# Half tiles of the hi and lo weight ring 2064 bytes apart in place of 2048

## The reference, cut to what matters

```python
split(xn @ w_in)                                   # 4096 x 5456 with the gate's low-rank part
for o, wb in zip((o_a, o_b, o_c, o_d), split(w_branch)):
    gate = sigmoid((z @ gate_up[i]))               # 256 x 4096 each
    merged = merged + gate * (o @ wb)              # 512 (or 256) x 4096 each
h = h + merged @ w_out                             # 4096 x 4096
q = xn2 @ wq                                       # 4096 x 1024
act = gelu(xn2 @ u.T)                              # 4096 x 4096
h = h + wmat @ v                                   # 4096 x 4096
```

## Time and profile before

| | |
|---|---|
| median of 2 runs | 1907.89 us (1907.87 to 1907.91) |
| span of the profiled execution, first to last instruction | 1906.1 us |
| TensorE matmul busy | 1900.6 us, 8941 recorded |
| TensorE weight load busy | 1567.2 us, 8941 recorded |
| VectorE busy | 1463.9 us |
| ScalarE busy | 984.9 us |
| TensorE's granted clock | 1.000 on average |

### The profile page before, as it was taken

How to read it: one execution, slowest core, us unless ns; L and a number is a source line. 1 busy time by engine, 2 the same in 40 slices (tenths; PEclk the granted TensorE clock), 3 DMA queues, 4 the chain that set the end, 5 groups by cost and what they waited for, 6 DMA issues and landing times.

```text
span 1906.1 us, 25847 instructions
## 1 busy us (share of the span) xinstructions
PE 1900.6 (100%) x8941; PEld 1567.2 (82%) x8941; DVE 1463.9 (77%) x2139; ACT 984.9 (52%) x1214; POOL 36.2 (2%) x49
## 2 busy tenths in 40 slices
PE   9999999999999999999999999999999999999999
PEld 8888888888888888888888888888887788888887
DVE  7578775584556889889765555899988878999897
ACT  6653644445456655546454464444444455555553
POOL 0010010000000000000000000000000000000000
PEclk9999999999999999999999999999999999999999
DMA  9976666655655668877887776767766668666664
GB/s 326 344 226 166 172 174 199 176 156 157 191 177 178 185 190 288 278 226 238 254 256 234 216 226 218 232 208 221 219 201 198 197 208 290 223 213 218 210 219 155
DMA packets 198832, 412.69 MB, mean 217 GB/s; under 512 B 45792, under 2 KB 124256, under 8 KB 198080
## 3 DMA queue, kind: packets, MB, share of 16 engines
q1 hardware_dynamic: 174048, 369.35, 63.0%
q10 hardware_dynamic: 20976, 25.19, 3.9%
q0 software_dynamic: 3696, 16.65, 2.4%
HBM read 390.15 MB, written 20.97 MB: 216 GB/s over the span
## 4 chain that ended last, share of the span: by engine, by line
PE 97%; DVE 2%; DMA 0%; issue 0%; ACT 0%; SPq 0%; DVEq 0%; ACTq 0%
PE acc L676 25%; PE acc L679 25%; PE acc L683 25%; PE acc L724 3%; PE acc L726 3%; PE acc L730 3%; PE side L1039 1%; PE side L1038 1%; PE acc L1152 1%; PE side L1040 1%; PE acc L1079 1%; PE acc L1085 1%; PE side L854 1%; PE acc L1080 1%; PE side L966 1%; DVE w_lo L1608 1%
## 5 line engine op out<-in xcount | busy, mean ns | idle before, releaser
L1608 DVE TENSOR_TENSOR w_lo<-w_raw,w_hi 128x1024 fp32r<-128x1024 f32 (+1 forms) x649 | 785.6, 1214 | 389.7 <-ACT w_hi L1199 384.9
L1199 ACT ACTIVATE w_hi<-w_raw 128x1024 fp32r<-128x1024 f32 (+1 forms) x649 | 681.1, 1052 | 701.2 <-PE acc L683 577.5
L676 PE MATMUL acc<-w_hi,xt_hi 128*128 128x512 f32 x1348 | 365.7, 393 | 0.0
L679 PE MATMUL acc<-w_hi,xt_lo 128*128 128x512 f32 x1348 | 360.8, 390 | 0.0
L683 PE MATMUL acc<-w_lo,xt_hi 128*128 128x512 f32 x1348 | 360.6, 389 | 0.0
L679 PEld LDWEIGHTS acc<-w_hi,xt_lo 128*128 128x128 f32 x1348 | 253.1, 188 | 53.1
L683 PEld LDWEIGHTS acc<-w_lo,xt_hi 128*128 128x128 f32 x1348 | 253.1, 188 | 52.9
L676 PEld LDWEIGHTS acc<-w_hi,xt_hi 128*128 128x128 f32 x1348 | 250.2, 188 | 51.5 <-issue 1.8
L676 PE MATMUL acc<-w_hi,x_hi 128*128 128x512 f32 x640 | 175.1, 396 | 0.0
L679 PE MATMUL acc<-w_hi,x_lo 128*128 128x512 f32 x640 | 171.5, 390 | 0.0
L683 PE MATMUL acc<-w_lo,x_hi 128*128 128x512 f32 x640 | 171.4, 390 | 0.0
(11 more groups left out here) (376 smaller groups left out, 2061.5 us busy)
## 6 DMA issues: line engine op xcount, KB each, us to landing
w_raw<-in_stream SPq DMA_DIRECT2D x504, 512.0 KB, 4.2
w_raw<-in_w_in SPq DMA_DIRECT2D x16, 496.0 KB, 4.1
w_raw<-in_w_in SPq DMA_DIRECT2D x16, 480.0 KB, 3.9
w_raw<-in_w_in SPq DMA_DIRECT2D x16, 464.0 KB, 3.8
w_raw<-in_w_in SPq DMA_DIRECT2D x16, 448.0 KB, 3.9
w_raw<-in_w_in SPq DMA_DIRECT2D x16, 432.0 KB, 3.9
w_raw<-in_w_in SPq DMA_DIRECT2D x16, 416.0 KB, 4.0
w_raw<-in_w_in SPq DMA_DIRECT2D x16, 400.0 KB, 3.8
```

The lines of the kernel that those rows point to most:

```text
L676: pe.matmul(o[h], lhs(k0 + j, h)[0], wh[j], start=first and j == 0, stop=False)
L679: pe.matmul(o[h], lhs(k0 + j, h)[1], wh[j], start=False, stop=False)
L1199: nc.scalar.activation(w_hi[:, slot, 0:width], w_raw[:, slot, 0:width], ACT.Copy).then_inc(hi_ready, 1)
L1608: nc.vector.tensor_tensor(w_lo[:, slot, 0:width], w_raw[:, slot, 0:width], w_hi[:, slot, 0:width].bitcast(F32), ALU.subtract).then_inc(lo_ ...
```

## The change

The half tiles of `w_hi` and `w_lo` get 516 numbers of room each, 2064 bytes, of which 512 are used. `w_raw` stays as it was, so ScalarE and VectorE now read one run of 1024 numbers and write two runs of 512 (for VectorE the second operand `w_hi` is in two runs as well). The first group's halves get the same places, so there half `j = 1` stands 2064 bytes behind `j = 0`, no longer 1344.

The ring grows by 16 x 16 = 256 bytes. All tiles from `MG0` on move up by 256 bytes; the tile `small` shrinks by 64 numbers (206 of its 320 were used), so that `PJ0` and what follows keep their addresses.

With 16 half tiles (4 slots, 2 halves, hi and lo) in a row, number n starts at n x 2064 bytes, so 16 x n bytes over a multiple of 2048, n from 0 to 15. Against stationary tiles at multiples of 512 the distances over a multiple of 512 are then 0, 16, 32, ... 240; against the few that moved with `MG0` they are the same less 256. Within a chunk TensorE reads hi j=0 twice, hi j=1 twice, the same four again, then lo j=0 twice and lo j=1 twice: the distance changes by 16 bytes between halves, by 128 between hi and lo, and by 32 from a slot to the next. The order of instructions on every engine is the same before and after; only the forms of the ScalarE and VectorE instructions named above differ.

```diff
 RING = 4
 LEAD = RING - 1
+HALF = 512 + 4
...
-    MG0 = RG0 + 12 * RING * KB
+    MG0 = RG0 + 4 * RING * KB + 4 * RING * HALF * 4
...
     w_raw = at("w_raw", [P, RING, 1024], F32, RG0)
-    w_hi = at("w_hi", [P, RING, 1024], F32R, RG0 + 4 * RING * KB)
-    w_lo = at("w_lo", [P, RING, 1024], F32R, RG0 + 8 * RING * KB)
+    w_hi = at("w_hi", [P, RING, 2, HALF], F32R, RG0 + 4 * RING * KB)
+    w_lo = at("w_lo", [P, RING, 2, HALF], F32R, RG0 + 4 * RING * KB + 2 * RING * HALF * 4)
...
-    small = const("small", [P, 320])
+    small = const("small", [P, 256])
...
+    def in_halves(row):
+        return row.rearrange("p (j n) -> p j n", j=2)
...
-                wh = [w_hi[:, slot, j * width:(j + 1) * width] for j in range(2)]
-                wl = [w_lo[:, slot, j * width:(j + 1) * width] for j in range(2)]
+                wh = [w_hi[:, slot, j, 0:width] for j in range(2)]
+                wl = [w_lo[:, slot, j, 0:width] for j in range(2)]
...
-                nc.scalar.activation(w_hi[:, slot, 0:width], w_raw[:, slot, 0:width], ACT.Copy).then_inc(hi_ready, 1)
+                nc.scalar.activation(w_hi[:, slot, :, 0:width // 2], in_halves(w_raw[:, slot, 0:width]), ACT.Copy).then_inc(hi_ready, 1)
...
-                nc.vector.tensor_tensor(w_lo[:, slot, 0:width], w_raw[:, slot, 0:width],
-                                        w_hi[:, slot, 0:width].bitcast(F32), ALU.subtract).then_inc(lo_ready, 1)
+                nc.vector.tensor_tensor(w_lo[:, slot, :, 0:width // 2], in_halves(w_raw[:, slot, 0:width]),
+                                        w_hi[:, slot, :, 0:width // 2].bitcast(F32), ALU.subtract).then_inc(lo_ready, 1)
```

More of the change, by code:

```diff
@@ L714, in branch_products @@
                 pe.wait_ge(hi_ready, chunk + 1)
-                wh = [w_hi[:, slot, j * 512:(j + 1) * 512] for j in range(2)]
-                wl = [w_lo[:, slot, j * 512:(j + 1) * 512] for j in range(2)]
+                wh = [w_hi[:, slot, j, 0:512] for j in range(2)]
+                wl = [w_lo[:, slot, j, 0:512] for j in range(2)]
                 for h in range(NT):
@@ L1042, in ring @@
             def ring(slot):
-                return [[w[:, slot, j * 512:(j + 1) * 512] for j in range(2)] for w in (w_hi, w_lo)]
+                return [[w[:, slot, j, 0:512] for j in range(2)] for w in (w_hi, w_lo)]
             def wait_block(pair, i, h):
@@ L1117, in last_products @@
                     for j in range(2):
-                        wh, wl = (w[:, slot, j * 512:(j + 1) * 512][:, cols] for w in (w_hi, w_lo))
+                        wh, wl = (w[:, slot, j, cols] for w in (w_hi, w_lo))
                         xh, xl = xt(2 * kp + j, 1)
@@ L1557, in hi_half @@
                 act.wait_ge(chunk_used, chunk - (RING - 1))
-                nc.scalar.activation(w_hi[:, slot, 512:1024], w_raw[:, slot, 512:1024], ACT.Copy).then_inc(hi_ready, 1)
+                nc.scalar.activation(w_hi[:, slot, 1, 0:512], w_raw[:, slot, 512:1024], ACT.Copy).then_inc(hi_ready, 1)
             def s_hi_part(i):
@@ L2282, in lo_half @@
                 dve.wait_ge(hi_ready, chunk + 1)
-                nc.vector.tensor_tensor(w_lo[:, slot, 512:1024], w_raw[:, slot, 512:1024],
-                                        w_hi[:, slot, 512:1024].bitcast(F32), ALU.subtract).then_inc(lo_ready, 1)
+                nc.vector.tensor_tensor(w_lo[:, slot, 1, 0:512], w_raw[:, slot, 512:1024],
+                                        w_hi[:, slot, 1, 0:512].bitcast(F32), ALU.subtract).then_inc(lo_ready, 1)
             def block_rows_of(pair, i, h):
```

## The result

The changed kernel takes 1945.36 us (median of 2 runs, 1945.18 to 1945.54) against 1907.89: a ratio of 1.0193, 95% interval 1.0176 to 1.0209. It is slower, by 37.5 us; whether by more than 2% the interval leaves open. The time lies inside the predicted range of 1860 to 1955, but not where the forecast of no change stood (1900 to 1917).

The account below looks back on a forecast made before the run. TensorE's back-to-back matmuls were taken to bound the kernel, their start-to-start time being what counts. Profiled span 1906.1 + 0 + 0 + 0, and 1.8 us around it, gave 1908 us; range 1860 to 1955.

Parts of the forecast that it names:

- no change: Whole kernel: the main forecast, time stays at 1908 us (1900 to 1917); chance 0.43.
- what bounds the kernel, and that only the interval between matmuls can move: TensorE: 97% of the chain of waits; only matmul start-to-start time counts, 226.7 ns each at 512 columns.
- ScalarE and VectorE at nothing: 649 copies and 649 subtractions in two runs: subtraction 0 us, copy at most +10 ns each, hidden by the ring.
- By this row the cost of another distance is 0: First group's 336-column chunks, half the matmuls at 320 over a multiple of 512, still pay 13.3 ns extra each.
- I take 0, since the 336-wide group alternates between two distances: Distance term for 7,700 matmuls set at 0, between bounds of -83 us and +69 us.
- a fixed price of a weight load: Each fp32r matmul pays 13.3 ns, 32 clock cycles, over its columns, whatever its width, with one weight load each.
- It never settles: Every ring matmul: shifting distances keep TensorE in uneven intervals, +4.2 ns each, 32 us, 1940 us; chance 0.27.
- Bad distances: Ring matmuls: offsets that are no multiple of 64 collide more, +9 ns each, 1977 us; chance 0.15.
- the uneven first chunk: First 512-wide chunk before the change: 2.77 us against 2.72 settled, 230.8 ns per matmul, without any wait.
- Faster, by a collision of tiles that lie alike: Multiples of 512 are the bad distances; 1825 us if all extra went, 1866 if half the matmuls; chance 0.15.
- one cycle for each 16-byte line of the stationary tile whatever its address: Stationary tile's 32 lines of 16 bytes explain the extra 32 cycles; addresses then don't matter, giving 1908 us.
- The working space 256 bytes up: Some `t` and `s` tiles of the fast steps shift: fewer than 400 matmuls, at most 9 ns each, taken as 0.

Follow-up runs that it names:

- k_cut448: Kernel before, but plain-product matmuls except each group's very first stream 448 of 512 columns, leaving 64 out of the sums: 1796.44 us; 12 matmuls in 2.43 us.
- g_slot64: Changed kernel with each slot 64 bytes further up than the last (distances 0, 64, 128, 192), one distance within a chunk: 1939.68 us.
- i_slots256: Changed kernel with the four slots at distances 256, 320, 384 and 448 over a multiple of 512, one per chunk: 1939.98 us.
- a_const16: Changed kernel with all sixteen half tiles 2048 bytes apart again, the whole 16 bytes further up, one distance for every ring matmul: 1942.31 us.
- b_lo16: Changed kernel with half tiles at multiples of 2048 bytes and only w_lo 16 bytes further up, both halves and all slots alike: 1934.16 us.
- c_half16: Changed kernel with only half j=1 16 bytes further up, in w_hi and w_lo alike, so distance alters after every second matmul: 1943.81 us.
- l_slots48: Changed kernel with the four slots 48, 96, 160 and 240 bytes over a multiple of 256, one distance per chunk: 1955.35 us.
- f_const32: Changed kernel with all half tiles 2048 bytes apart again, the whole 32 bytes further up, one distance for every ring matmul: 1953.34 us.
- e_const64: Changed kernel with all half tiles 2048 bytes apart again, the whole 64 bytes further up, one distance for every ring matmul: 1924.69 us.
- h_all32: Kernel before with every tile, stationary ones too, 32 bytes further up, so addresses change but all distances stay: 1909.13 us.
- m_slots80: Changed kernel with the four slots 80, 112, 208 and 224 bytes over a multiple of 256, one distance per chunk: 1942.62 us.

## Why the prediction was wrong where it was

- **Right: what bounds the kernel, and that only the interval between matmuls can move.** 97% of the chain is TensorE as before; 36.5 of the 37.1 us lie in the intervals of ring matmuls.
- **Right: ScalarE and VectorE at nothing.** 1060 ns against 1059, 1222 against 1223. Nobody waits longer for them.
- **The step that failed: "By this row the cost of another distance is 0", and "I take 0, since the 336-wide group alternates between two distances".** It took one width for another. Matmuls of 336 columns average 153.3 ns at 16, 32 or 64 alone as with 0 and 320 in turn, and also with the changed kernel's distances, so that row could not show the price that 512 columns pay. What the row did show, that 336 columns pay the same 13.3 ns as 512, was then read as a fixed price of a weight load. `k_cut448` shows that it isn't one (16.0 ns at 448 columns). With that the ground for "no change" is gone. The term for the distance should have been +4.9 ns x 7,500 (the ring's matmuls of 512 columns), 37 us, not 0. Nor did the row test much: by `g_slot64` and `i_slots256` 320 acts as 64, one of the cheaper distances.
- **That the range held the time is owed to the rivals.** "No change" had 0.43, "It never settles" 0.27 and "Bad distances" 0.15; the range of 1860 to 1955 was drawn wide enough to take in the second.
- **The rival "It never settles" had the size: +4.2 ns, 1940 us, against +4.9 and 1945.** Its price came from the uneven first chunk. Its reason is half right. `a_const16` loses 34.4 us with a single distance that never alters, so most of the loss does not need the altering; `b_lo16` and `c_half16` take 15 and 19 us more than their static shares, so the altering has a price too. In the changed kernel both are mixed and no run parts them exactly. An estimate from the table, each distance weighted by how often the changed kernel reads at it (128, 144 and 176, which the table lacks, taken as the mean of the others from 160 to 240; where the table has two numbers, their mean), is 232.0 ns, and 232.1 were measured: here the prices of the distances alone nearly give the loss.
- **"Bad distances" expected +9 ns.** The mechanism is there: single distances that are no multiple of 64 cost, and its sign, intervals that differ by slot with the same pattern every four chunks, is what the changed kernel shows (2790, 2794, 2784, 2778 ns and again 2790). Only the size was too high: the dearest distance tried alone (32) costs +6.6 ns, and about +10 (240) was seen only at the ends of single chunks of `l_slots48`. Nor is a multiple of 64 free: 64 costs +2.3.
- **Faster, by a collision of tiles that lie alike: no.** 0 is the best of the distances tried.
- **The Trainium skill** (SBUF — State Buffer, "Who interferes with whom") calls TensorE's two read ports independent and says that TensorE never waits on anyone. Here shifting one of the two tiles by 32 bytes costs 45 us and shifting both by 32 costs 1: for fp32r the time does depend on how the two tiles lie to each other, and the measurement decides. The other reading of the prediction, one cycle for each 16-byte line of the stationary tile whatever its address, falls by `k_cut448` and by `f_const32` (48 cycles at the same 32 lines).
- **The working space 256 bytes up was taken as 0.** By the period of 256 its own distance is as before. Yet the 372 recorded matmuls with `t` tiles went from 226.8 to 230.7 ns, 1.4 us, and nearly as much in `e_const64` (230.4), while `h_all32` left them at 226.8. They stand in groups of up to 12 between ring matmuls, and in the changed kernel the first of a group averages 233.9 ns and the eleventh and twelfth 226.8 and 226.6: they pay for the change of distance and then settle. No run moves the working space alone.

What stays open is the mechanism: what the two reads share, why the picture repeats after 256 bytes, and why 512 columns at distance 0 give the shortest rhythm. At 128 the chunks of `g_slot64` and `i_slots256` end before a rhythm is seen, 144 and 176 stand only in the changed kernel, and a distance of no multiple of 16 was not tried.

## What to carry to other kernels

When fp32r matmuls, each with its own weight load, follow each other without a gap, compare their start-to-start time with the columns over the clock, and try the byte distance between the moving and the stationary tiles: here, for 512 columns, a multiple of 256 in place of one other distance was worth 0.9% of the time (against 64) to 2.3% (against 32). Keep it the same for all tiles of a ring. And don't carry a price from one width to another: the width that seemed to prove that distance is free was one at which 16, 32 and 64 cost the same.

## What the runs showed of the hardware

- Without any wait, TensorE falls into exactly repeating rhythms: one interval (226.7 ns = 544 cycles at 2.4 GHz) at distance 0, three intervals at 64, four at 16, five with 448 columns. The sums over 12 matmuls in steady chunks, 2720, 2780, 2746.7 and 2800 ns for 0, 16, 64 and 32, are 408, 417, 412 and 420 times 16 cycles, within rounding; so are four chunks of the changed kernel (11,146 ns, 1672 times). Single uneven chunks are not (2777 ns is 416.5 times). That hints at a step of 16 cycles somewhere in this path; it is a reading of these sums, and no run tests it.
- One distance can have two rhythms: 112 bytes gave 2.72 and 2.77 us for the same 12 matmuls, in turn in the first chunks of `m_slots80`.
- The order of best and worst depends on the width: at 512 columns distance 0 beats 16 by 5.0 ns, at 256 columns 16 beats 0 by 3 ns (11 intervals each), and at 336 a distance of 16, 32 or 64 gives the same 153.3 ns (0 alone was not run at that width).
